# Moving three quarters of the weighted sums of gathered value rows from VectorE to fp32 products on TensorE, in a two-block transformer kernel

## What is computed

```python
def peer_ffn(x, w_peer_q, peer_subkeys, peer_u, peer_v):
    q = (x @ w_peer_q).reshape(B, S, 8, 2, 128)
    s = jnp.einsum('bshcd,hcnd->bshcn', q, peer_subkeys)
    top_s, top_i = lax.top_k(s, 16)
    ...                                   # 16 best of the 16x16 sums: experts, best_s
    gates = jax.nn.softmax(best_s, axis=-1)
    act = jax.nn.gelu(jnp.einsum('tkd,td->tk', peer_u[experts], x))
    return jnp.einsum('tk,tkd->td', gates * act, peer_v[experts])
...
    h = h + peer_ffn(rms_norm_2(h, ffn_norm[l]), ...)
    gate = jax.nn.sigmoid(rms_norm_2(h, ple_norm[l]) @ w_ple_gate[l])
    h = h + gate * (p[l] @ w_ple_proj[l])
return rms_norm_2(h, final_norm)
```

## Time and profile before

| | |
|---|---|
| median of 3 runs | 4106.8 us (4105.35 to 4119.67) |
| the profiled execution's own time | 4102.67 us |
| its span, first to last instruction | 4100.9 us |
| TensorE, matmuls | 2564.1 us busy, 63% |
| VectorE | 2921.1 us busy, 71% |
| ScalarE | 1309.2 us busy, 32% |
| GpSimd | 1082.3 us busy, 26% |
| mean granted TensorE clock | 0.812 of 2.4 GHz |
| bytes moved by gathers (queue 0) | 536.9 MB of 953 MB |

### The profile page before, as it was taken

The page is one execution under the profiler, slowest core; times in us unless marked ns, Lnnn a source line. Parts: engine busy times, 40 slices in busy tenths (PEclk is TensorE's granted clock), DMA queues, the critical chain, the costliest instruction groups (busy, mean ns, idle before and its releaser), DMA issues.

```text
span 4100.9 us, 50118 instructions
## 1 busy us (share of the span) xinstructions
PE 2564.1 (63%) x19730; PEld 2455.5 (60%) x19730; DVE 2921.1 (71%) x3488; ACT 1309.2 (32%) x1780; POOL 1082.3 (26%) x516
## 2 busy tenths in 40 slices
PE   8999798999999999899998986400000000000028
PEld 8888687999999999899996986400000000000028
DVE  5667755654455458654655658899999999999985
ACT  4355444553454445544454442300000000000023
POOL 0000000000000000000000001377767778888850
PEclk9999899999999999999999998755555555555569
DMA  6433243555555564455451547899999999999974
GB/s 216 131 121 114 72 130 118 173 183 186 179 185 185 179 196 145 150 182 183 152 186 43 185 150 288 299 352 355 353 349 353 351 349 400 420 421 418 421 289 133
DMA packets 187579, 952.96 MB, mean 232 GB/s; under 512 B 20816, under 2 KB 21072, under 8 KB 121424
## 3 DMA queue, kind: packets, MB, share of 16 engines
q0 software_dynamic: 73728, 536.90, 33.7%
q1 hardware_dynamic: 112464, 407.68, 31.0%
q10 hardware_dynamic: 1152, 5.17, 0.3%
HBM read 947.58 MB, written 2.10 MB: 232 GB/s over the span
## 4 chain that ended last, share of the span: by engine, by line
PE 54%; DVE 28%; POOL 11%; issue 3%; ACT 3%; DMA 1%; DVEq 0%; ACTq 0%; SPq 0%; POOLq 0%
PE ps L420 53%; POOL BIG L408 9%; DVE HF L1959 8%; DVE BIG L1943 7%; POOL HF L408 2%; DVE HL L1403 2%; DVE BIG L1407 1%; DVE HF L1943 1%; DVE TMP L1403 1%; DVE BIG L1403 1%; DVE TMP L1407 1%; PE ps L424 1%; ACT BIG L909 0%; DVE TMP L1897 0%; DVE TMP L1890 0%
## 5 line engine op out<-in xcount | busy, mean ns | idle before, releaser
L420 PE MATMUL ps<-HS,HL 128*128 128x256 f32 x11936 | 1528.5, 288 | 68.5 <-DVE HL L1403 51.7
L420 PEld LDWEIGHTS ps<-HS,HL 128*128 128x128 f32 x11936 | 1492.9, 196 | 83.8 <-DVE HL L1403 55.6
L408 POOL DMA_INDIRECT BIG<-in_peer_u,CS x211 | 408.9, 1938 | 2717.3 <-DVE CS L1411 2470.9
L1403 DVE TENSOR_TENSOR HL<-RAW,HL 128x1024 fp32r<-128x1024 f32 (+1 forms) x772 | 939.5, 1217 | 222.9 <-ACT HL L915 160.5
L915 ACT CAST HL<-RAW 128x1024 fp32r<-128x1024 f32 (+1 forms) x772 | 805.1, 1043 | 632.2 <-PE ps L420 587.7
L424 PE MATMUL ps<-CON,HF 128*128 128x128 f32 x32 | 7.3, 373 | 1333.1 <-DVE HF L1959 1332.1
L424 PEld LDWEIGHTS ps<-CON,HF 128*128 128x128 f32 x32 | 5.4, 193 | 1335.4 <-issue 1293.3
L420 PE MATMUL ps<-BIGR,HL 128*128 128x256 f32 x5680 | 745.2, 285 | 1.5 <-DVE BIGR L1403 1.5
L420 PEld LDWEIGHTS ps<-BIGR,HL 128*128 128x128 f32 x5680 | 707.9, 192 | 7.8 <-issue 3.7
L1943 DVE CUSTOM_DVE_ANT_0 BIG<-BIG 128x2048 f32<-128x2048 f32 x211 | 483.7, 2292 | 39.9 <-DMA BIG<-in_peer_u,CS 19.6
L1959 DVE SCALAR_TENSOR_TENSOR HF<-BIG,GA,HF 128x2048 f32<-128x2048 f32 x204 | 479.6, 2351 | 22.3 <-DMA BIG<-in_peer_v,CS 1.0
(11 more groups left out here) (160 smaller groups left out, 1763.2 us busy)
## 6 DMA issues: line engine op xcount, KB each, us to landing
RAW<-in_w_up SPq DMA_DIRECT2D x128, 512.0 KB, 3.7
RAW<-in_w_down SPq DMA_DIRECT2D x128, 512.0 KB, 4.2
RAW<-in_w_out SPq DMA_DIRECT2D x64, 512.0 KB, 3.4
RAW<-in_w_qk SPq DMA_DIRECT2D x32, 512.0 KB, 4.3
RAW<-in_w_xbc SPq DMA_DIRECT2D x32, 512.0 KB, 3.3
RAW<-in_w_xr SPq DMA_DIRECT2D x32, 512.0 KB, 3.4
RAW<-in_w_yr SPq DMA_DIRECT2D x32, 512.0 KB, 3.5
RAW<-in_w_gr SPq DMA_DIRECT2D x32, 512.0 KB, 4.2
```

The costliest lines, as they stand in the source:

```text
L408: e.indirect_dma_start(out=ROWS[slot], out_offset=None, in_=A["peer_" + table], in_offset=bass.IndirectOffsetOnAxis(ap=EX[:, i, 16 * h + k ...
L420: return e.matmul(o, l, r, start=start, stop=stop, skip_group_check=True)
L1403: v.done(e.tensor_tensor(o, a, b, op), sig)
```

## The change

- The items are ordered by halves: n = 8 i + h, so half 0 is complete after item 7.
- `gathers` alternates. The first 32 rows are u rows; from then on u and v rows take turns (15 v to 14 u), as long as the gates of the item are there; the last 16 rows are the v rows of item 15.
- `by_vector(g)` says who uses a row: VectorE all u rows and every fourth v row (k = 3, 7, 11, 15), that is 256 + 64; TensorE the other 192 v rows.
- For each of these 192 rows ScalarE writes a diagonal matrix with the tokens' gates (128x128, one of four buffers DIAG), and TensorE multiplies it with the row: four fp32 products 128x512 that add up in four PSUM banks, which the half keeps until its end. The row's buffer is free when the last of the four is done (s_pused).
- At the end of a half VectorE adds the four banks to its own ACC (`joined`), TensorE turns the sum, VectorE adds it to X (`added`), ScalarE squares it and TensorE sums the squares. For half 0 this stands between rows of half 1, for half 1 behind the last row.
- `score_bank` use "acc" and the 8 groups of squares of `ple_norm` go.

```diff
         def gates(n):
-            h, i = divmod(n, 2)
+            i, h = divmod(n, 8)
...
-        gathers = [("u", 0, k) for k in range(16)]
-        for n in range(1, 16):
-            gathers += [("u", n, k) for k in range(16)] + [("v", n - 1, k) for k in range(16)]
-        gathers += [("v", 15, k) for k in range(16)]
+        us, vs = [[(x, n, k) for n in range(16) for k in range(16)] for x in ("u", "v")]
+        gathers = []
+        for a in range(256):
+            gathers.append(us[a])
+            while vs and a >= 16 * vs[0][1] + 17 and (256 - len(vs)) * 224 < (a - 31) * 240:
+                gathers.append(vs.pop(0))
+        gathers += vs
+        def by_vector(g):
+            return g[0] == "u" or g[2] % 4 == 3
...
                 if before is not None:
-                    e.wait_ge(s_used, before + 1)
+                    e.wait_ge(s_vused if by_vector(gathers[before]) else s_pused, turn[before])
...
-            for j in range(8):
-                k = SCORE["acc"] + j
...
+            def value(q, n, k):
+                i, slot, p = n // 8, place[q][0], turn[q]
...
+                pe.wait_ge(s_diag, p)
+                pe.wait_ge(s_row[slot], 16 * place[q][1])
+                for b in range(4):
+                    m = mm(PS[4 - 4 * i + b][:, :], DIAG[(p - 1) % 4], ROWS[slot][:, 512 * b:512 * b + 512], n % 8 + k == 0,
+                           n % 8 == 7 and k == 14)
+                m.then_inc(s_pused, 1)
...
+            for q, (table, n, k) in enumerate(gathers):
                 g, d, r = gates(n)
-                s.wait_ge(s_ext, n + 1)
-                act(g, g, ACT.Exp, (s_gexp, n + 1), acc=r[:, 0:1])
-                s.wait_ge(s_used, taken["u", n, 15] + 1)
-                act(d, d, ACT.Gelu_apprx_tanh, (s_gact, n + 1))
+                if table == "u" and k == 15:
+                    s.wait_ge(s_ext, n + 1)
+                    act(g, g, ACT.Exp, (s_gexp, n + 1), acc=r[:, 0:1])
+                    s.wait_ge(s_vused, turn[q])
+                    act(d, d, ACT.Gelu_apprx_tanh, (s_gact, n + 1))
+                if not by_vector(gathers[q]):
+                    s.wait_ge(s_gates, n + 1)
+                    if turn[q] > 4:
+                        s.wait_ge(s_pused, turn[q] - 4)
+                    act(DIAG[(turn[q] - 1) % 4], con("ident"), ACT.Identity, (s_diag, turn[q]), scale=g[:, k:k + 1])
+                if q in (HALF0 + 12, HALF0 + 20):
+                    for j in range(2):
+                        half_square(0, j + 2 * (q == HALF0 + 20))
...
+            def joined(i, b):
+                v.wait_ge(s_pused, turn[taken["v", 8 * i + 7, 14]])
+                o = ACC[:, i, 512 * b:512 * b + 512]
+                tt(o, o, PS[4 - 4 * i + b][:, :], ALU.add, (s_acc, 4 * i + b + 1))
...
+                for q, (table, n, k) in enumerate(gathers):
+                    if q in gate_at:
+                        while not late[0]:
                             yield
-                        else:
-                            step(routes)
+                        gated(gate_at[q])
+                    if table == "u":
+                        while found[0] <= n:
...
+                        dot(q, n, k)
+                        step(routes)
+                    elif by_vector(gathers[q]):
+                        value(q, n, k)
```

More of the change, by code:

```diff
@@ L283, in gates @@
         def gates(n):
-            h, i = divmod(n, 2)
-            o = 384 + 2 * (8 * i + h)
+            i, h = divmod(n, 8)
+            o = 384 + 2 * n
             return GA[:, i, 16 * h:16 * h + 16], DOT[:, i, 16 * h:16 * h + 16], SM[:, o:o + 2]
-        gathers = [("u", 0, k) for k in range(16)]
-        for n in range(1, 16):
-            gathers += [("u", n, k) for k in range(16)] + [("v", n - 1, k) for k in range(16)]
-        gathers += [("v", 15, k) for k in range(16)]
[L294 to L298, removed]
+        us, vs = [[(x, n, k) for n in range(16) for k in range(16)] for x in ("u", "v")]
[5 more added lines that the diff above has]
+        gathers += vs
+        taken = {g: q for q, g in enumerate(gathers)}
+        def by_vector(g):
+            return g[0] == "u" or g[2] % 4 == 3
+        place, used, turn, seen = [], [[] for _ in ROWS], [], [0, 0]
+        for q, g in enumerate(gathers):
+            b = q % 4 if q < 32 else (q + 2) % 5
+            place.append((b, len(used[b]) + 1, used[b][-1] if used[b] else None))
+            used[b].append(q)
+            seen[by_vector(g)] += 1
+            turn.append(seen[by_vector(g)])
+        HALF0 = taken["v", 7, 15]
         s_con, s_vec, s_pos, s_mem = sem("con_in"), sem("vec_in"), sem("positions_in"), sem("mem_in")
@@ L886, in tensor @@
[L886 to L887 removed]
+            def value(q, n, k):
+                i, slot, p = n // 8, place[q][0], turn[q]
+                if (n, k) == (0, 0):
+                    pe.wait_ge(s_sfree[0], SCORE["score"] // 2 + 4)
+                    pe.wait_ge(s_sfree[1], SCORE["score"] // 2 + 4)
+                    pe.wait_ge(s_tfree, TURN["rows"] + 8)
+                    pe.wait_ge(s_ofree, OUTS["mla"] + 16)
+                if (n, k) == (8, 0):
+                    for c in (13, 14, 15):
+                        bank_done(L["w2_pp"], c)
+                    pe.wait_ge(s_nfree, NORM["ple_norm"])
+                pe.wait_ge(s_diag, p)
[4 more added lines that the diff above has]
+                m.then_inc(s_pused, 1)
@@ new lines, in turned_values, with half_sum @@
+            def turned_values(i, j):
+                pe.wait_ge(s_acc, 4 * i + 4 if i == 0 else 5 + j)
+                if j >= 2:
+                    pe.wait_ge(s_tbf, 4 * i + j - 1)
+                for c in range(4):
+                    p = tr(PS[4 + j % 2][:, 128 * c:128 * c + 128], ACC[:, i, 512 * j + 128 * c:512 * j + 128 * c + 128])
+                p.then_inc(s_tb, 1)
+            def half_sum(i, j):
+                q = SQ["ple_norm"] + 4 * i + j
+                pe.wait_ge(s_square, q + 1)
+                for c in range(4):
+                    p = mm(PS[7][:, 128 * i:128 * i + 128], con("ones"), SQT[j % 2][:, c, :], j + c == 0, j == 3 and c == 3)
+                p.then_inc(s_sq, 1)
@@ L889, in gated @@
+            for j in range(4):
+                turned_values(1, j)
+                if j >= 2:
+                    half_sum(1, j - 2)
+            half_sum(1, 2)
+            half_sum(1, 3)
             def gated(c):
@@ L1937, in arrived, with dot, gated @@
                 v.prev()
[L1938 to L1942, removed]
+                return ROWS[slot], (s_vused, turn[q])
+            def dot(q, n, k):
+                i, h = divmod(n, 8)
+                row, sig = arrived(q)
                 v.done(e.tensor_tensor_reduce(row, row, HN[:, i, :], 1.0, 0.0, ALU.mult, ALU.add,
                                               DOT[:, i, 16 * h + k:16 * h + k + 1]), sig)
-            def values(n):
-                h, i = divmod(n, 2)
+            def gated(n):
                 g, d, r = gates(n)
@@ L1951, in values, with value, added @@
                 v.wait_ge(s_gact, n + 1)
[L1952 to L1957, removed]
-                    else:
-                        v.done(e.scalar_tensor_tensor(out=ACC[:, i, :], in0=row, scalar=c, in1=ACC[:, i, :], op0=ALU.mult,
-                                                      op1=ALU.add), sig)
-                    yield
+                stt(g, g, r[:, 1:2], d, ALU.mult, ALU.mult, (s_gates, n + 1))
+            def value(q, n, k):
+                i, h = divmod(n, 8)
+                row, sig = arrived(q)
+                c = GA[:, i, 16 * h + k:16 * h + k + 1]
+                if h == 0 and k == 3:
+                    v.done(e.tensor_scalar(ACC[:, i, :], row, c, None, ALU.mult), sig)
+                else:
+                    v.done(e.scalar_tensor_tensor(out=ACC[:, i, :], in0=row, scalar=c, in1=ACC[:, i, :], op0=ALU.mult,
+                                                  op1=ALU.add), sig)
+            def joined(i, b):
+                v.wait_ge(s_pused, turn[taken["v", 8 * i + 7, 14]])
+                o = ACC[:, i, 512 * b:512 * b + 512]
+                tt(o, o, PS[4 - 4 * i + b][:, :], ALU.add, (s_acc, 4 * i + b + 1))
+            def added(i, j):
+                v.wait_ge(s_tb, 4 * i + j + 1)
+                x = X[:, 4 * j:4 * j + 4, 128 * i:128 * i + 128]
+                tt(x, x, PS[4 + j % 2][:, :].rearrange("p (c t) -> p c t", c=4), ALU.add, (s_tbf, 4 * i + j + 1))
             def chain():
@@ L1967, in experts @@
             def experts():
-                routes, ready = chain(), []
+                routes, gate_at = chain(), {}
+                for n in range(16):
+                    gate_at[max(taken["u", n, 15] + 3, 32) if n < 15 else taken["u", 15, 15] + 1] = n
                 while not rowed[0]:
                     yield
-                for n in range(16):
-                    while found[0] <= n:
-                        if pq[0] < n // 2 * 2 + 2:
```

(35 more changed lines are left out.)

56 lines of the change are left out of this document (37 added, 19 removed).

## The result

4081.5 us, the median of 11 runs (4063.7 to 4099.4), against 4106.8 before: ratio 0.9929, 95% interval 0.9914 to 0.9944. The direction was right, but the forecast was 3977 with a range of 3938 to 4045, and of its 130 us 25 (medians) to 29 (ratio) came.

A forecast was written before the change was run, and what follows sets the result against it. VectorE was taken to bound the first part, VectorE and DMA nearly together the second. Gathers -128, end +2 and -4 made -130 us: 4102.7 to 3973, with the median 4 above at 3977; range 3938 to 4045.

The forecast's parts named there:

- the first part: Gathers up to 3376 us, where VectorE also routes: 2.976 us a row, said to be limited by VectorE alone.
- The row on TensorE: Four fp32 products 128x512 for a v row: 3.41 us at full clock, 6.83 at half.
- Routing: VectorE's routing steps, 0.94 us each: said to run ahead of the dots, so s_ext never comes late.
- the DMA limit: Price of a gathered row with DMA as only limit: 2.49 us taken, 2.43 as lower end, 128 us saved.
- The end: After the last gather: 2.3 us more until its rows are used, then 4 us less to the first `w2_pg` product.
- Buffers: Five-buffer loop of 12.45 us against 6.9 held plus 5.3 shortest landing, 12.2: said to be just in time.
- The full bad case: Buffers without margin, second row cold too: 0.25 us more per row, 2.74; half of it gave the upper end's 2.62.
- The sign of being wrong: One of the signs named: POOL waiting for TensorE rows more than 2 us in eight gathers.
- TensorE's clock: Of each three TensorE rows, 6.83, about 3.9 and 3.41 us: 14.2 of 19.9 us, covered by the gathers.
- half clock throughout: Rival: TensorE at half clock for all 192 rows, 1311 us; total 4091, within 0.5% of before; 8%.
- The rival of weight loads: Rival: TensorE's loads of the diagonals are not hidden, 9.6 us a row, total about 4620; 5%.
- GpSimd's lock-step: GpSimd's 2.15 us gather instructions read as waiting for VectorE's long ones, so shorter, down to 0.94, with gaps on VectorE.

The follow-up runs named there:

- e1: The changed kernel with only the first of the four products of each TensorE row, output incomplete: 3995.4 us, 0.9715 of the kernel before.
- e13: The changed kernel with six row buffers from gather 33 and seven from gather 161: 3995.2 us, 0.9703 of the kernel before.
- e2: The changed kernel with six row buffers in place of five from gather 160 on: 4020.7 us, 0.9789 of the kernel before.
- e5: The changed kernel with every second v row on VectorE, 128 left to TensorE, five buffers: 4132.4 us, 1.0044 of the kernel before.
- e9: The split of e5 plus five unused filler products behind each TensorE row, item 15 excepted: 4078.0 us, 0.9919 of the kernel before.
- e15: The changed kernel with VectorE's dots over only half the columns, so half of every dot is missing: 4048.5 us, 0.9837 of the kernel before.
- e10: The changed kernel plus unused products after TensorE rows: one, or four where VectorE takes the next; none in item 15: 4058.9 us, 0.9864.

## Why the prediction was wrong

**What held.** VectorE was the limit of the first part and is no longer: 358 us of 1150 fewer than in the same stretch before (722 against 1080, the DVE figure of this row of before):

```profile
2700.00:3850.00 1150.00, 0.00 (x0) 0.00 (x0) 1080.38 (x1040) 40.18 (x65) 907.90 (x416) 0.50 0.97 377
```

The row on TensorE costs what was worked out, 3.44 us at full clock (the last gathers wait for it, 3.43 apart); the first of each three, forecast at 6.83, took 5.8 on average and 6.7 at most, the second and third 3.65 and 3.7. Routing came early enough, the DMA limit was 2.47 to 2.50, as e1 and e13 show. ScalarE takes 0.40 us a diagonal, and in e13, with the same diagonals, nothing of it shows; in the change TensorE waited for a diagonal 11 times in the stretch, 23.7 us in all and once for 6.8, and what that cost with five buffers was not separated. The end was right too: last gather to the last product 14.0 us (13.5 forecast), from there to `w_pg` 14.4 (14.2), and last gather to the end of the span 144.6 us where it was 145.3.

**What failed is the step "Buffers".** It set the loop of five buffers, 12.45 us, against a hold of 6.9 and the shortest landing in the trace, 5.3, and found it "just in time". The hold was sized well enough, at 5.2 to 6.7 us. What was wrong is the landing, and it was the smallest number of a row whose median in the full part was 9.0. Measured, a landing takes 8.6 to 9.0 us in the median; even where the gather went out after more than 4 us of idleness on POOL, the seven landings on record are 5.8 to 8.1 us, 7.0 in the median. With 7.0 the step would have read 6.9 + 7.0 = 13.9 us against a loop of 12.45, which is too late; measured, the loop is 5 x 2.716 = 13.6 us, of which some 8.8 are landing and 4.8 are use and waiting. One buffer more takes the loss away without touching a hold (e2, e13).

**And a limit forgives no gap.** The step reckoned with averages: TensorE busy 14.2 of 19.9 us, hence "covered". But the transfers were to run at 2.49 with 2.47 as their floor. Every gap in them is lost, as there is no faster pace at which to make up for it. The full bad case stood in the text (2.74 a row), and 2.716 was measured; I took half of it for the upper end without a row that said so. That 2.74 and 2.716 are so close is luck: the bad case had the second row at half clock too, and it took 3.65 us on average. With 2.74 the sum would have been 479 x 2.74 = 1312 and the time about 4096. The sign of being wrong that was named, POOL waiting for TensorE more than 2 us in eight gathers, came (364 us in 424 gathers, 6.9 in eight), but it is no good sign: e13 has 6.2 in eight and runs at the limit.

**TensorE's clock** played its part as forecast in kind: a row behind a gap took 5.8 us on average, and the granted clock was 0.82. The rival "half clock throughout" (4091) came near in time, but by another way: TensorE was busy 62%, and not the limit, so that nearness is chance. The rival of weight loads is refuted by the 3.44 us a row. The Trainium skill's "TensorE: Matmul & The Clock Gate", Part 1, with the half clock for an engine that is not kept busy, agrees with these rows: 0.82 here, 0.72 in e5, 0.94 in e9.

**GpSimd's lock-step** with VectorE was read rightly: where VectorE has gaps the median instruction takes 0.94 us, and under two long VectorE instructions in a row it takes 2.96 and 2.13 (3013.95 and 3017.22 above). The prediction counted this as a gain only; it also slows GpSimd when it has gathers to catch up with, at a price of 20 us at most (e15).

## What to carry to other kernels

When work moves to a slower engine, ask how long each buffer is held, not only whether the engine has time: the rate of a ring is the number of buffers over landing plus hold, with the landing as it is in a full queue, and an issuer that works in order hands one late release on to all behind it. At the limit of a transfer engine, average slack elsewhere is no cover; a queue of issued transfers is, and here, by the ratios, one more buffer from gather 161 on was worth 57 us (0.9929 to 0.9789) and one or two more over the whole stretch 93 (to 0.9703). Look for memory that is free for part of a stage, such as the sum of a half that has not begun.

## What the runs showed that was not expected

- Giving TensorE a third less work cost 47 us (e5), with its clock at 0.72, and giving it more work that computes nothing gave 51 back (e9). With filler in both, the smaller share on TensorE was still some 20 us slower (e9 against e10).
- The share of busy DMA engines hardly tells starvation: 0.98 at 387 GB/s, 1.00 at 417. The interval between gathers does.
- The median of the kernel before was 4105 to 4120 in different sets of runs, so only ratios within a set are compared. The start of gather 33, before which nothing was changed but the order of items, lay between 2634 and 2651 us in the profiled executions, e15 aside; what sets it was not tried.
